# A gather split in three and spread over the first expert's weights, in a two-block transformer kernel

## The reference

```python
def one_group(hs):                        # hs: 272 x 1024, normed rows
    aff = jax.nn.softmax(hs @ w_router, axis=-1)          # 272 x 16
    g, idx = lax.top_k(aff.T, cap)                        # cap = 34
    xg = hs[idx]                                          # 16 x 34 x 1024
    a = jnp.einsum('ecd,edf->ecf', xg, w_gate)            # 16 x 1024 x 2048 weights
    u = jnp.einsum('ecd,edf->ecf', xg, w_up)              # 16 x 1024 x 2048
    y = jnp.einsum('ecf,efd->ecd', jax.nn.silu(a) * u, w_down)   # 16 x 2048 x 1024
    return jnp.zeros((L, D)).at[idx.reshape(-1)].add((y * g[..., None]).reshape(-1, D))
```

## Time and profile before

| | |
|---|---|
| median of three timed executions | 1636.78 us (1636.6 to 1639.06) |
| the profiled execution, from first to last instruction | 1637.3 us |
| PE busy | 1480.3 us, 90% of the span |
| DVE, ACT, POOL busy | 553.1, 415.5, 118.5 us |
| DMA traffic | 511.49 MB, mean 312 GB/s |
| expert stage, from the first gather to the last down matmul | about 166 to 1072 us |
| chain that ended last | PE 60%, DMA 31%, DVE 6% of the span |

### The profile page before, as it was taken

The page is one execution under the profiler, slowest core; times in us unless marked ns, Lnnn a source line. Parts: engine busy times, 40 slices in busy tenths (PEclk is TensorE's granted clock), DMA queues, the critical chain, the costliest instruction groups (busy, mean ns, idle before and its releaser), DMA issues.

```text
span 1637.3 us, 18705 instructions
## 1 busy us (share of the span) xinstructions
PE 1480.3 (90%) x7823; PEld 885.9 (54%) x7823; DVE 553.1 (34%) x957; ACT 415.5 (25%) x823; POOL 118.5 (7%) x121
## 2 busy tenths in 40 slices
PE   9999999987888888888878879899999999999999
PEld 8874433322322222222223223278889899988887
DVE  6754100100101001001001001078875565878843
ACT  5522100000000000000000000066733655456532
POOL 2011000000000000000000000050520200600000
PEclk9998999999999999999999999999999999999999
DMA  9436899999999999999999999955332334555564
GB/s 380 186 130 252 359 428 430 429 431 432 429 431 432 430 431 430 430 431 430 431 430 431 432 429 430 421 183 189 129 106 82 129 117 156 190 170 184 190 194 140
DMA packets 44468, 511.49 MB, mean 312 GB/s; under 512 B 5200, under 2 KB 5456, under 8 KB 27616
## 3 DMA queue, kind: packets, MB, share of 16 engines
q1 hardware_dynamic: 42624, 506.10, 76.1%
q10 hardware_dynamic: 1760, 4.19, 0.8%
HBM read 509.23 MB, written 1.05 MB: 312 GB/s over the span
## 4 chain that ended last, share of the span: by engine, by line
PE 60%; DMA 31%; DVE 6%; ACT 1%; issue 1%; POOL 0%; ACTq 0%; SPq 0%; DVEq 0%; POOLq 0%
DMA sb_ring<-in_w_gate_up 28%; PE PS L757 12%; PE PS L824 9%; PE PS L796 9%; PE PS L1212 6%; PE PS L858 4%; PE PS L891 3%; DMA sb_ring<-in_w_down 2%; PE PS L664 2%; PE PS L857 2%; PE PS L775 2%; PE PS L968 1%; PE PS L516 1%; PE PS L524 1%; DVE sb_wp L2165 1%
## 5 line engine op out<-in xcount | busy, mean ns | idle before, releaser
L757 PE MATMUL PS<-sb_ring,sb_XG 128*64 128x512 f32 x2048 | 478.9, 623 | 104.0 <-DMA sb_ring<-in_w_gate_up 104.0
L757 PEld LDWEIGHTS PS<-sb_ring,sb_XG 128*64 128x64 f32 x2048 | 152.6, 143 | 423.8 <-issue 276.4
L2184 DVE TENSOR_TENSOR sb_SL<-sb_SL,PS 128x512 f32<-128x512 f32 x32 | 20.6, 684 | 788.8 <-PE PS L757 788.8
L796 PE MATMUL PS<-sb_ring,sb_HT 128*64 128x512 f32 x1024 | 234.0, 615 | 19.6 <-DVE sb_HT L2198 6.9
L2165 DVE TENSOR_TENSOR sb_wp<-sb_raw,sb_wp 128x1024 fp32r<-128x1024 f32 x157 | 199.1, 1270 | 95.5 <-ACT sb_wp L1415 94.6
L1415 ACT CAST sb_wp<-sb_raw 128x1024 fp32r<-128x1024 f32 x160 | 166.8, 1046 | 106.6 <-PE PS L1212 55.5
L796 PEld LDWEIGHTS PS<-sb_ring,sb_HT 128*64 128x64 f32 x1024 | 86.0, 142 | 157.3 <-issue 130.7
L824 PE MATMUL PS<-sb_hr,sb_wp 128*128 128x256 f32 x1200 | 151.2, 285 | 0.3 <-DVE sb_wp L2165 0.3
L824 PEld LDWEIGHTS PS<-sb_hr,sb_wp 128*128 128x128 f32 x1200 | 145.8, 192 | 3.8 <-issue 3.2
L1427 ACT ACTIVATE sb_SL<-PS 128x512 f32<-128x512 f32 x32 | 17.4, 595 | 513.3 <-PE PS L757 513.3
L858 PE MATMUL PS<-sb_hr,sb_wp 128*128 128x512 f32 x256 | 87.8, 396 | 0.0
(11 more groups left out here) (421 smaller groups left out, 1416.3 us busy)
## 6 DMA issues: line engine op xcount, KB each, us to landing
sb_ring<-in_w_gate_up SPq DMA_DIRECT2D x55, 4096.0 KB, 40.1
sb_ring<-in_w_down SPq DMA_DIRECT2D x27, 4096.0 KB, 41.0
sb_raw<-in_w SPq DMA_DIRECT2D x160, 512.0 KB, 3.3
sb_ring<-in_w_gate_up SPq DMA_DIRECT2D x15, 2048.0 KB, 9.6
sb_ring<-in_w_down SPq DMA_DIRECT2D x9, 2048.0 KB, 13.8
sb_ring<-in_w_in SPq DMA_DIRECT2D x12, 1024.0 KB, 16.5
sb_ring<-in_w_gate_up SPq DMA_DIRECT2D x6, 1024.0 KB, 9.6
sb_ring<-in_w_out SPq DMA_DIRECT2D x4, 1024.0 KB, 13.9
```

Of the source, the lines that this page charges most:

```text
L757: ins = e.matmul(PS[64 * g:64 * g + 64, b, :], m.XG[:, k, r0:r0 + 64], m.ring[s][:, (2 * g + q) * 512:(2 * g + q) * 512 + 512], start=(k = ...
L796: ins = e.matmul(PS[64 * g:64 * g + 64, b, :], m.HT[:, c % 8, (c // 8) * 64:(c // 8) * 64 + 64], m.ring[s][:, a * 1024 + g * 512:a * 1024 ...
```

## The change

Three edits are made together.

1. The columns of `S` are made and gathered in three parts, experts 0 and 1 (68 columns), 2 to 7 (204) and 8 to 15 (272), in place of two of 272. Part 0 of chunks 0 and 1 stands ahead of expert 0's first gate and up matmuls, and part 0 of chunk k + 1 ahead of those of chunk k. Parts 1 and 2 stand where the table `LATER` puts them: for chunk 0 ahead of k = 3, for chunks 1 and 2 ahead of k = 4, 3 and 4 ahead of 5, 5 and 6 ahead of 6, 7 ahead of 7.
2. Expert 0's matmuls of chunk k wait only for part 0 of it, expert 1's for parts 1 and 2. ACT copies parts 0 and 1, DVE part 2. Part 0 uses banks 4 and 5, part 1 bank 6, part 2 bank 7.
3. Pieces 36 and 37 are brought in two transfers of 1 MB.

```diff
-HALVED = (28, 52, 16 + 24 * 16 - 10, 16 + 24 * 16 - 2)
+HALVED = (28, 36, 52, 16 + 24 * 16 - 10, 16 + 24 * 16 - 2)
...
+GATHERED = ((0, 2), (2, 8), (8, 16))
+LATER = ((), (), (), (0,), (1, 2), (3, 4), (5, 6), (7,))
...
-    def gather(c):
-        for half in range(2):
-            b = room((4, 6)[c % 2] + half, "xg", c, half)
...
+    def gather(c, part):
+        e0, e1 = GATHERED[part]
+        b = room(4 + c % 2 if part == 0 else 5 + part, "xg", c, part)
+        for ti in range(2):
+            pe.wait_ge(*at("xn hi", ti))
+            pe.wait_ge(*at("xn lo", ti))
+            pe.wait_ge(*at("slots", part))
+            for q in range(2):
+                ins = e.matmul(PS[:, b, 0:CAP * (e1 - e0)], m.XNp[q][ti][:, c * 128:c * 128 + 128], m.S[:, ti, e0:e1, :],
+                               start=(ti == 0 and q == 0), stop=(ti == 1 and q == 1))
+        ins.then_inc(*mark("pe_moe", "in", "xg", c, part))
...
             if ex == 0:
                 if k < 7:
-                    gather(k + 1)
-                pe.wait_ge(*at("xg pad"))
+                    gather(k + 1, 0)
+                for c in LATER[k]:
+                    gather(c, 1)
+                    gather(c, 2)
                 pe.wait_ge(*at("out", "xg", k, 0))
-                pe.wait_ge(*at("out", "xg", k, 1))
+            elif ex == 1:
+                if k == 0:
+                    pe.wait_ge(*at("xg pad"))
+                for part in (1, 2):
+                    pe.wait_ge(*at("out", "xg", k, part))
...
-    gather(0)
+    gather(0, 0)
...
+    gathered(0, 0)
+    for k in range(8):
+        if k < 7:
+            gathered(k + 1, 0)
+        for c in LATER[k]:
+            gathered(c, 1)
...
-    for half in range(2):
-        e0, e1 = 8 * half, 8 * half + 8
+    for part, (e0, e1) in enumerate(GATHERED):
         for ti in range(2):
...
-        dve.wait_ge(*at("in", "xg", c, 1))
-        e.tensor_copy(m.XG[:, c, 272:544], PS[:, banks.of("xg", c, 1), 0:272]).then_inc(*mark("dve_moe", "out", "xg", c, 1))
+        dve.wait_ge(*at("in", "xg", c, 2))
+        e.tensor_copy(m.XG[:, c, 272:544], PS[:, banks.of("xg", c, 2), 0:272]).then_inc(*mark("dve_moe", "out", "xg", c, 2))
```

More of the change, by code:

```diff
@@ L1415, in hi, with gathered @@
             e.copy(m.wp_hi[n % WR], m.raw[raw_turn(n) % RAW]).then_inc(*mark("act_split", "hi", n))
[L1418 to L1421, removed]
+    def gathered(c, part):
+        e0, e1 = GATHERED[part]
+        act.wait_ge(*at("in", "xg", c, part))
+        e.copy(m.XG[:, c, CAP * e0:CAP * e1], PS[:, banks.of("xg", c, part), 0:CAP * (e1 - e0)]).then_inc(*mark("act_moe", "out", "xg", c, part))
+    gathered(0, 0)
[4 more added lines that the diff above has]
+            gathered(c, 1)
     for ex in range(NE):
@@ L2152, in dve_program @@
     dve.wait_ge(*now("dve_route"))
-    for half in range(2):
-        e0, e1 = 8 * half, 8 * half + 8
+    for part, (e0, e1) in enumerate(GATHERED):
         for ti in range(2):
-            e.tensor_tensor(m.S[:, ti, e0:e1, :], bc(m.iota[:, 0:CAP], 1, 8), bc(m.ps[:, ti, e0:e1], 2, CAP), ALU.is_equal).then_inc(*mark("dve_route", "slots", half, ti))
+            event = ("slots", part) if ti else ("slots half", part)
+            e.tensor_tensor(m.S[:, ti, e0:e1, :], bc(m.iota[:, 0:CAP], 1, e1 - e0), bc(m.ps[:, ti, e0:e1], 2, CAP), ALU.is_equal).then_inc(*mark("dve_route", *event))
     dve.wait_ge(*at("xn lo", 1))
```

## The result

The changed kernel takes 1641.43 us in the median of 13 executions (1638.64 to 1642.05), the kernel before 1638.22 beside it (13, 1635.3 to 1641.93). The ratio is 1.0018, 95% interval 1.0010 to 1.0025: 2.9 us slower, between 1.6 and 4.1. Forecast were 1638.6 and a slowdown of 1.8. The rest is the change's own, 1.1 us by the ratio.

The account below looks back on a forecast made before the run. The expert stage was taken as bound by the weight stream, then PE. PE's 5.2 us more less 1.5 at the start gave D 3.7; less 1.9 in hand, +1.8 us on 1637.3, minus 0.5: 1638.6, range 1635.4 to 1640.8.

Parts of the forecast that it names:

- cheap-matmul rival: Gathers of expert 0: short matmuls cost 0.03 and 0.094 us, D is 0.7, stream 1.2 us earlier, 1635.6; chance 0.16.
- the banks: Double gathers: second chunk waits for both copies in full, stream 3.9 to 4.8 us later, 1640.7 to 1641.6; chance 0.08.
- D: How much later PE comes to places in expert 0 from 205.9 on: 5.2 - 1.5 = 3.7 us.
- The tightest place is 54/55 with 1.9 us in hand: Weight transfer 54/55, in expert 0's down matmuls: 0.8 MB still queued at its readiness, so at most 1.9 us gain passes.
- the change is worth 1.9 - D: Stream behind 54/55: PE D us later there makes it late by D - 1.9, forecast 3.7 - 1.9 = +1.8 us.
- On the way the stream does not suffer more: Expert 0's steps: despite about 1 us idle ahead of chunks 1, 4, 5, 6, not later at 50/51 (3.7 against 3.9).
- share 1.00 throughout leaves no hidden reserve: Stream around 54/55: DMA engines always busy, so it cannot go on there; argument against 3.3 us of gain arriving.
- the first rival: Expert 0's down matmuls: clock stays up, D there 2.3, stream only 0.4 us later, 1637.2; chance 0.22.
- The gain passes after all: Rival at 54/55: its reserve an artefact of unevenly filled engines, the 3.3 us earlier issue arrives, 1633.5; chance 0.04.
- the stream is later: Main case: stream behind 54/55 is 1.8 us later and stays so to the kernel's end, 1638.6; chance 0.40.
- The rival on the stage's end: Last 64 gate and up records: shifted clock falls give back 1.5 to 3 us, 1635.6 to 1637.1; chance 0.10.
- restart theory: Follow-up theory, expert 0's stream: each time the queue runs dry, engines restart late and unevenly, costing some 0.3 to 0.8 us.

Follow-up runs that it names:

- e1: The kernel before with pieces 36 and 37 in two transfers of 1 MB, nothing else: 1638.63 against 1638.32 us, ratio 1.0001.
- e12: The kernel before, unchanged, run once more for a second profile: 1637.62 us, ratio 0.9998.
- e8: The changed kernel without parts 1 and 2 (rows of experts 2 to 15 zeros): 1635.93 against 1637.85 us for the kernel before, ratio 0.9987.
- e4: The changed kernel with three parts only for chunks 0 and 1, chunks 2 to 7 in halves: 1636.69 us, ratio 0.9990 to the kernel before.
- e6: The kernel before with 32 repeated gather matmuls more, ahead of chunks 0 and 1: 1641.27 us, ratio 1.0014.
- e10: The changed kernel with chunks 0 to 3 in three parts (1 and 2 ahead of chunks 6 and 7), others halved: 1639.49 us, 1.0007 to before.
- e9: The changed kernel with all parts 1 and 2 ahead of chunks 6 and 7: 1639.84 against 1638.00 us for the kernel before, ratio 1.0003.
- e13: The kernel before, unchanged, one profile more: one execution, 1637.23 us.
- e15: The same kernel as e4, timed again on another chip: 1637.61 against 1638.96 us for the kernel before, ratio 0.9992.
- e16: The same kernel as e1, for a second profile: one execution, 1637.98 us.
- e11: The changed kernel, unaltered, run again for a second profile: 1640.31 us, ratio 1.0017 to the kernel before.
- e14: The changed kernel, unaltered, for a third profile: one execution, 1641.26 us.
- e3: The changed kernel with parts 1 and 2 of one chunk ahead of every chunk: 1640.76 us, ratio 1.0015 to the kernel before.

## Why the prediction missed

**What held.** Gate and up began 1.5 us earlier, as worked out. Eight short matmuls cost 0.11 each, so the cheap-matmul rival fell, and the banks took the small share given them. D at 50/51 was 3.95 us for a forecast 3.7, of which the steps are 5.4 for 5.2. ACT's table load kept its cover; timeline of ACT after, with the last gate matmuls of chunk 7 begun at 205.71:

```profile
205.65 1.28 ACT L1444 ACT_TABLE_LOAD   x1
207.69 1.09 ACT L1444 ACTIVATE sb_SL<-PS 128x512 f32<-128x512 f32 x2 [0.76 <-PE PS L766]
```

The stream ran full from 222 to the stage's end, and what it had lost there arrived 1:1 at 1041.87. Direction and chain were right.

**The step that failed** is the one on how much of the gap can be won, "The tightest place is 54/55 with 1.9 us in hand" and "the change is worth 1.9 - D", with the two sentences that guarded it, "On the way the stream does not suffer more" and "share 1.00 throughout leaves no hidden reserve". 54/55 was issued 2.5 us later, not 3.7: expert 0's down matmuls ran at full clock, which is the first rival's condition. By my rule the stream would be 0.6 us later (the rival itself had 0.4, 1637.2); it was 2.8 later in that very profile. That my forecast of 1.8 isn't further off is luck: D was 1.2 us too large, and the loss on the way, which I had at nothing, was larger than that. And 54/55 was no place where the stream stood: 2.1 us of bytes were queued at its readiness, more than before. At 50/51 the queue of 0.46 MB (14.68 - 361 x 39.4) would have been through at 61.6 behind piece 29, before at 60.6: 1.0 us later already, where I had it not later at all. The other 1.8 were lost between 211 and 223, with PE issuing in time and the share at 0.98 to 1.00.

The sign stood in my own rows: the earlier trace rows has 401 to 410 GB/s at a share of 1.00, where the earlier trace rows has 431, and the fifth slice of the earlier trace rows, which I called full, has 359. I had taken bytes in hand as time in hand, divided by 431 GB/s. In the full stream, at 431 GB/s throughout, the two are the same. After a dry spell they weren't: the packets below show some engines slow while others run at the usual pace, so I take it that the bytes in hand lay in the engines that lagged. No record tells the engines apart. The steps over 4.87 us, which I let pass because the later place seemed tighter, are what costs: 2.0 us of idle engines, and 4 us more than before in which they were busy and moved too little.

**What was off in size.** The baseline, 1.4 us (result section). Of the 3.3 us of the earlier issue I had counted PE's 1.5, and the 1.8 of the single transfers at nothing. In e1 that held (started 1.6 us earlier than e12, lost 1.8 more). But by the windows e8 keeps all of the 3.3, and e4 a third of it. "The gain passes after all" and "the stream is later" were both true, with a larger loss than either held. The rival on the stage's end was right in kind: 15.43 us in place of 16.89.

**What stays open.** How much of the loss is the restarts and how much is only PE's lateness: the windows show the loss in every profile, but of the restart theory's sizes those for e6, e8 and e10 missed. Whether the restarts alone make e9 less slow than the change: the difference is near what the runs resolve. Whether the 10.2 us of low clock ahead of the first gather is likelier with three parts: it was so in 9 of 10 profiles of such kernels and in 3 of 8 of the others. e12 and e13, e4 and e15, e1 and e16 are pairs of the same kernel, and each pair shows both lengths, so it goes by the execution; whether the odds differ isn't settled, and at most 1.4 us hang on it. So the forecast -1.5 at the start holds between executions of one kind, and is next to nothing between kinds (e12 18.4, changed kernel 18.3). Parts 1 and 2 during expert 0's down matmuls or in expert 1, where PE waits for the stream anyway, weren't tried: `XNp` lies in memory that expert 0's activation and hidden values use.

## What to carry to other kernels

Price a stream of transfers as first issue plus what it loses until it is full, and read the loss from GB/s, not from the busy share: length x (1 - GB/s / full rate). Work that is moved off the start of a stream should go where the kernel has a gap in its own feeding (here ahead of chunk 7) and in no more pieces than needed: each step that takes PE longer than the DMA engines need for its two pieces (4.9 us for 2 MB) lets them run dry and, in these profiles, costs more than the idle time shown. A short matmul behind a full weight load costs almost as much as one four times as wide, so a gather cut in three is paid for in matmuls, 96 for 64.

## What the runs showed of the hardware

**Engines that start again lag and get uneven.** In the transfer records of the traces, a 16 KB packet takes 0.61 us where the stream is full. The first ones of before after the dry spell at 169 to 173 took 1.1 to 1.4, single ones up to 2.4. In the changed kernel ten of the 16 packets begun between 211.4 and 212.1 took 1.6 to 1.9 us, the others 0.6 to 0.8; 50/51 had been ready in time, and the rate from 211 to 215 was 320 GB/s. Between the issue of 36 and 70 us later there were about 120 packets of more than 1.5 times the usual length in the changed kernel and about 45 before; e8 had about as many as before, and the other two profiles of the changed kernel about 125 and 130. The excess of all packets over the usual time, spread over the 16 engines, is 6.3 us for each in the changed kernel (6.1 and 5.6 in e11 and e14), 2.4 before. That is the difference of 4 that the windows show too. Why a first packet takes so long no run here shows.

The Trainium skill ("DMA: Bandwidth & Descriptors", Latency and other measured facts) puts an access to HBM at 0.2 us on average and 2 us at high load. The long packets here come when the load has just been nil, so that rule alone doesn't tell them.

**The row for my short matmul ran partly at the low clock.** Windows of before over the 48 matmuls of the earlier trace rows, 0.109 each:

```profile
149.90:155.20 5.30, 5.27 (x50) 5.11 (x48) 2.61 (x7) 2.91 (x8) 0.55 (x1) 0.79 0.98 400
```

and of e12, the same kernel, where the clock fell later:

```profile
149.60:153.90 4.30, 4.29 (x51) 4.13 (x48) 2.60 (x7) 2.27 (x8) 0.55 (x1) 1.00 0.98 398
```

Timeline of PE in e12:

```profile
149.66 4.24 PE L707 MATMUL PS<-sb_vec,sb_hnT 128*128 128x16 f32 x48
```

At full clock 16 columns take 0.088 us. The 0.11 for 68 and 204 columns, here at clock 1.00, was right by luck: the row that I had for it was a mean over two clocks. The granted clock of a row belongs beside its duration.

With this the sentence of the prediction falls by which the trace's 0.109 agrees with the 107 ns that the Trainium skill ("TensorE: Matmul & The Clock Gate", LDWEIGHTS) gives for a full weight load. At full clock, 16 columns are nearer to the 81 ns that its Back-to-back issue gap section gives for loads with matmuls of 128 columns, while the 0.11 of 68 and 204 columns in the changed kernel stays near the 107 ns of the first.

**The clock's falls come and go.** Expert 0's down matmuls ran at the low clock (0.51) for 3.4 us in the profile of before and in e3 and e10, of eighteen profiles (some 15.4 against 13.95 us); neither e12 nor e13, the same kernel, showed it.
